# A hybrid decoder block: nine modulation sections loaded transposed and summed along the row on VectorE

## The reference, cut to what matters

```
c_act = silu(c)                                   # 1024 numbers
mod   = c_act @ w_ada + b_ada                     # nine sections of 1024
sh1, sc1, gt1, sh2, sc2, gt2, sh3, sc3, gt3 = split(mod, 9)
x = x + 0.5*gt1*swiglu(rmsnorm(x)*(1+sc1)+sh1)    # first feed-forward
x = x + gt2*mixer(rmsnorm(x)*(1+sc2)+sh2)         # attention and short convolution
x = x + 0.5*gt3*swiglu(rmsnorm(x)*(1+sc3)+sh3)    # second feed-forward
shf, scf = split(c_act @ w_ada_final + b_ada_final, 2)
out = rmsnorm(x)*(1+scf)+shf
```

## Time and profile before

| | before |
|---|---|
| median of three runs | 1863.17 us |
| profiled execution, its time | 1860.78 us |
| profiled execution, its span | 1859.0 us |
| PE busy, of the span | 1810.6 us, 97% |
| DVE busy | 1261.2 us, 68% |
| ACT busy | 774.6 us, 42% |
| bytes moved | 269.77 MB, mean 145 GB/s |
| mean granted TensorE clock | 0.996 of 2.4 GHz |

### The profile page before, as it was taken

How to read it: one execution, slowest core, us unless ns; L and a number is a source line. 1 busy time by engine, 2 the same in 40 slices (tenths; PEclk the granted TensorE clock), 3 DMA queues, 4 the chain that set the end, 5 groups by cost and what they waited for, 6 DMA issues and landing times.

```text
span 1859.0 us, 23169 instructions
## 1 busy us (share of the span) xinstructions
PE 1810.6 (97%) x8370; PEld 1472.2 (79%) x8370; DVE 1261.2 (68%) x1951; ACT 774.6 (42%) x1393; POOL 268.3 (14%) x411
## 2 busy tenths in 40 slices
PE   6999999999999999999999999999999999999997
PEld 3778888888888887888877777778888888888886
DVE  5887777777576786444326668787667666576767
ACT  5643333333344565211125666663333333344445
POOL 2011211211210000000303330201111111111000
PEclk9999999999999999999999999999999999999998
DMA  8165565665765321111211110424545545476432
GB/s 324 58 235 205 200 231 193 225 216 181 266 215 155 106 69 70 56 34 57 68 38 42 46 35 1 176 97 159 196 170 181 207 153 193 159 261 215 125 97 91
DMA packets 100529, 269.77 MB, mean 145 GB/s; under 512 B 13120, under 2 KB 13504, under 8 KB 100288
## 3 DMA queue, kind: packets, MB, share of 16 engines
q1 hardware_dynamic: 65680, 150.50, 24.0%
q0 software_dynamic: 34304, 117.46, 18.5%
q10 hardware_dynamic: 432, 0.34, 0.1%
HBM read 209.53 MB, written 54.53 MB: 142 GB/s over the span
## 4 chain that ended last, share of the span: by engine, by line
PE 86%; DVE 8%; ACT 3%; issue 1%; DMA 1%; POOL 0%; ACTq 0%; DVEq 0%; POOLq 0%
PE PS L1554 62%; PE PS L1550 23%; DVE Wl L1021 1%; DVE NMax L1463 1%; PE PS L1988 1%; DMA AdaFirst<-ada 1%; DVE X L1359 1%; DVE X L1122 1%; ACT X L701 0%; ACT Bh L701 0%; DVE CT L1428 0%; DVE Bl L1128 0%; DVE SqSum L1328 0%; DVE Ml L1262 0%; DVE TmpA L1346 0%
## 5 line engine op out<-in xcount | busy, mean ns | idle before, releaser
L1554 PE MATMUL PS<-Bh,Wh 128*128 128x512 f32 x1120 | 437.5, 391 | 4.5 <-ACT T L684 4.1
L1554 PE MATMUL PS<-Bh,Wl 128*128 128x512 f32 x1120 | 435.9, 389 | 0.0
L1554 PE MATMUL PS<-Bl,Wh 128*128 128x512 f32 x1120 | 435.8, 389 | 0.0
L1554 PEld LDWEIGHTS PS<-Bh,Wh 128*128 128x128 f32 x1120 | 210.3, 188 | 50.7 <-DVE Wl L1021 4.9
L1554 PEld LDWEIGHTS PS<-Bh,Wl 128*128 128x128 f32 x1120 | 210.2, 188 | 44.0
L1554 PEld LDWEIGHTS PS<-Bl,Wh 128*128 128x128 f32 x1120 | 210.3, 188 | 43.1
L1554 PE MATMUL PS<-Wh 128*128 128x512 f32 x616 | 240.0, 390 | 0.0
L1554 PE MATMUL PS<-Wh,Wl 128*128 128x512 f32 x616 | 239.7, 389 | 0.0
L1554 PE MATMUL PS<-Wl,Wh 128*128 128x512 f32 x616 | 239.7, 389 | 0.0
L1053 DVE TENSOR_TENSOR Wl<-RawB,Wh 128x512 fp32r<-128x512 f32 x154 | 106.5, 692 | 130.3 <-ACT Wh L659 129.3
L659 ACT ACTIVATE Wh<-RawB 128x512 fp32r<-128x512 f32 x154 | 97.3, 632 | 230.7 <-PE PS L1554 230.7
(11 more groups left out here) (201 smaller groups left out, 2872.6 us busy)
## 6 DMA issues: line engine op xcount, KB each, us to landing
Raw<-up_w SPq DMA_DIRECT2D x86, 512.0 KB, 5.3
Ada<-ada POOLq DMA_DIRECT2D x72, 512.0 KB, 4.3
g_dram<-T SPq DMA_DIRECT2D x88, 256.0 KB, 2.3
W2s<-down_w POOLq DMA_DIRECT2D x88, 256.0 KB, 4.5
s_dram<-W2s POOLq DMA_DIRECT2D x88, 256.0 KB, 2.8
GQ<-g_dram POOLq DMA_DIRECT2D x88, 256.0 KB, 3.4
RawB<-s_dram SPq DMA_DIRECT2D x88, 256.0 KB, 2.9
RawB<-down_w SPq DMA_DIRECT2D x66, 256.0 KB, 2.7
```

The costliest lines, as they stand in the source:

```text
L1554: return nc.tensor.matmul(out, lhs, rhs, start=first, stop=last, skip_group_check=True)
```

## The change

Of the nine later sections the matrix is stored transposed, so that a tile has 128 outputs on its partitions and all 1024 inputs along the row. `silu(c)` is needed along the row as well: `c`, copied to all 128 partitions, is stored behind the tiles. In each phase SP loads it into `CRow` (half a megabyte), and ACT applies Silu to it in place. `CRow` lies where `AdaSum` lay, over the second half of an operand of the plain jobs and over `Spread`, so its load waits for both. A DVE instruction per tile then multiplies tile and `CRow` and gives the sum of the products along the row as its accumulator output, straight into one column of `Mod`; the products themselves overwrite the tile. `ada_cols` goes, and with it `ada_between`. `ada_bias` adds the bias to `Mod` in place.

```diff
@@ SP, block_of
-                for q in (0, 2, 1, 3):
+                for q in (0, 2):
+                    spill(ph, 0, q)
+                sp.wait_ge(prod, N_FFN * ph + 8)
+                sp.wait_ge(bcast_done, 2 + 4 * ph)
+                sp.dma_start(CRow[:], ada[SECTIONS * KT]).then_inc(row_loaded, 16)
+                for q in (1, 3):
                     spill(ph, 0, q)
@@ ACT, up
                     if t > 10:
                         up_evict(ph, t - 1)
+                    if t == 11:
+                        act.wait_ge(row_loaded, 16 * (ph + 1))
+                        nc.scalar.activation(CRow[:], CRow[:], ACT.Silu).then_inc(c_act, 1)
@@ DVE, ada_tile
+                if s in (ADA_IN[0][0], ADA_IN[1][0]) and k == 0:
+                    dve.wait_ge(c_act, 2 if s == ADA_IN[0][0] else 3)
                 dve.wait_ge(ada_loaded[n % 2], 16 * (n // 2 + 1))
-                if k == 0:
-                    dve.wait_ge(cols_done, s + 1)
-                    nc.vector.tensor_scalar(AdaSum[:], Ada[:, n % 2, :], CAct[:, 0:1], None, ALU.mult).then_inc(ada_used, 1)
-                else:
-                    dve.wait_ge(ada_used, s * KT + k)
-                    nc.vector.scalar_tensor_tensor(AdaSum[:], Ada[:, n % 2, :], CAct[:, k:k + 1], AdaSum[:],
-                                                   ALU.mult, ALU.add).then_inc(ada_used, 1)
+                a = s * KT + k
+                nc.vector.scalar_tensor_tensor(Ada[:, n % 2, :], Ada[:, n % 2, :], 1.0, CRow[:], ALU.mult, ALU.mult,
+                                               accum_out=Mod[:, a:a + 1]).then_inc(ada_used, 1)
@@ DVE, ada_bias
-                dve.wait_ge(cols_done, s + 2 if s else 2)
+                if s:
+                    dve.wait_ge(ada_used, (s + 1) * KT)
@@ PE, up
-                    ada_between(ph, t)
@@ PE
-            def ada_cols(s, bank=7):
-
-                pe.wait_ge(ada_used, (s + 1) * KT)
-                for c in range(KT):
-                    made = mm(PS[:, bank, c:c + 1], AdaSum[:, blk(c)], Ones[:], True, True)
-                made.then_inc(cols_done, 1)
@@ arrays
-        "ada": ada_w.reshape(KT, P, SECTIONS, D).transpose(2, 0, 1, 3).reshape(SECTIONS * KT, P, D),
+        "ada": np.concatenate([ada[:2 * KT], turned[2 * KT:], np.broadcast_to(a["c"][0], (1, P, D))]),
```

More of the change, by code:

```diff
@@ L189, in program @@
         Ada, _ = place("Ada", [P, 2, D], like=z_at)
-        AdaSum, _ = place("AdaSum", [P, D], like=z_at + 8 * K)
+        CRow, _ = place("CRow", [P, D], like=z_at + 8 * K)
         W2s, _ = place("W2s", [P, 4, HALF], like=tmp_at)
@@ L359, in program @@
         mset, consts, c_act = sem("mset"), sem("consts"), sem("c_act")
+        row_loaded = sem("row_loaded")
         ada_used, row_used, row_done = sem("ada_used"), sem("row_used"), sem("row_done")
@@ L1305, in second_scale, with ada_bias @@
                                                col("g1", KH * n, KH), ALU.add, ALU.mult).then_inc(scales, 1)
-            def ada_bias(s, bank=7):
-                dve.wait_ge(cols_done, s + 2 if s else 2)
-                nc.vector.tensor_tensor(Mod[:, bass.ts(s, KT)], PS[:, bank, 0:KT], Cols[:, bass.ts(s, KT)], ALU.add)\
-                    .then_inc(mod_done, 1)
+            def ada_bias(s):
+                if s:
+                    dve.wait_ge(ada_used, (s + 1) * KT)
+                else:
+                    dve.wait_ge(cols_done, 2)
+                nc.vector.tensor_tensor(Mod[:, bass.ts(s, KT)], Mod[:, bass.ts(s, KT)] if s else PS[:, 4, 0:KT],
+                                        Cols[:, bass.ts(s, KT)], ALU.add).then_inc(mod_done, 1)
             def scale(n, section, gain):
@@ L1398, in _ @@
             second_bias(0)
-            ada_bias(SH1, 4)
+            ada_bias(SH1)
             second_scale(0)
@@ L1559, in spin @@
                     mm(PS[:, bank, HALF - P:HALF], ident, ident, True, True)
[L1561 to L1567, removed]
             def plain_group(ph):
@@ L2091 @@
     below = np.where(np.arange(P)[None, :] <= np.arange(P)[:, None], 0.0, MASKED)
+    ada = ada_w.reshape(KT, P, SECTIONS, D).transpose(2, 0, 1, 3).reshape(SECTIONS * KT, P, D)
+    turned = ada_w.T.reshape(SECTIONS * KT, P, D)
     arrays = {
```

## The result

The changed kernel took 1845.28 us (median of four runs, 1843.78 to 1846.76) against 1863.16 before (1862.52 to 1863.54): ratio 0.9904, interval 0.9887 to 0.9922, 17.9 us less. The forecast was 1848.5 with a range from 1846.5: right in direction and mechanism, too small, and the time fell out of the range at its lower end. The profiled execution took 1845.61, 15.2 less than that of before.

The account below looks back on a forecast made before the run. TensorE was taken to bound the kernel, its chain in the up projections broken only by nine blocks. -15.7 + 0.7 + 0.3 = -14.7 us, from 1863.17 to 1848.5 us; range 1846.5 to 1856.

Parts of the forecast that it names:

- mechanism: Up projections: TensorE is the unbroken chain, so matmul blocks taken out of it are time spared at the end.
- The term of the blocks: TensorE, up projections: nine column-making matmul blocks at 1.68 to 1.81 us each go, 15.7 us gained.
- the stalls: TensorE waiting for DVE sums delayed by tiles: 0.7 us at the two first tiles, 0.3 at six later places.
- The tile's growth x: DVE: the accumulator output lengthens each 1.28 us tile by 0 to 1.06 us; 0.15 taken.
- The late matmul of the earlier trace: TensorE at t = 61, first matmul of j = 6: already late behind a DVE tile and sum, slack -0.2 us.
- the slack method: Compares when DVE's sum arrives with when TensorE wants it, wherever a tile stands ahead; 1.0 us lost in all.
- The rule against this change: DVE: two non-bf16 SBUF sources halve throughput, leaving no read port for accumulator readback; the sum would be rival 1's.
- Rival 1: DVE tiles: accumulator output halves the rate, x = 1.06; net gain 8.3 us, 1855 us; chance 0.11.
- Rival 2: Up projections: the nine blocks were covered by sums or weights, two thirds of the gain lost, 1858 us; chance 0.04.
- Rival 3: Phase 0 sections: DVE ends the up projections if tiles exceed 3.2 us; at 3.6 us, 1878 us; chance 0.03.
- Rival 4: Row's load lands late and ACT stops at t = 11: +0.6 us a phase, 1850 us; within the forecast's 0.80.
- What SP, the queues and ACT get: Row load issued at about 91.3, Silu from 104.3 to 105.4, both hidden; no cost to TensorE.

Follow-up runs that it names:

- later tiles: Changed kernel with eight identity matmuls ahead of t = 12 in phase 0 alone and each phase's first tile at t = 15 instead of 12: 1842.96 us.
- gap_spin: Changed kernel with eight identity matmuls (spins) on TensorE just ahead of t = 12 in both phases: 1843.86 us.
- blocks out: Kernel before without the nine blocks, with eight identity matmuls ahead of t = 12 in both phases: 1843.19 us.
- tile_pointer: Changed kernel with the tile's constant factor 1.0 read from a column of ones: 1845.81 us.
- blocks_back: Changed kernel with the nine blocks of eight matmuls put back at their old places on TensorE, result unread: 1862.10 us.
- after: The changed kernel itself against the kernel before, first measurement and its profile: 1845.28 us.
- after_again: The changed kernel measured once more without any edit: 1846.15 us.
- blocks_out: Kernel before without the nine blocks, tiles and sums as they were, no identity matmuls: 1845.36 us.
- tile_later: Changed kernel with the first tile of each phase at t = 15 in place of 12: 1844.59 us.
- spin_first: Changed kernel with eight identity matmuls ahead of t = 12 in phase 0 alone: 1844.59 us.

## Why the prediction was right or wrong

**The mechanism was right.** The blocks lay bare on the path, and their removal is the gain: blocks put back, 1862.10; blocks alone out, 1845.36. The rest of the change takes 0.3 us of it back.

**The term of the blocks was mis-sized: this is the step that failed first.** The gain was forecast as 14.7 us and measured as 17.9. Of the 3.2 between them 0.9 is this term, 0.7 the stalls (next paragraph), and the other 1.6 is chance in the main (last two paragraphs). It says "Nine blocks are 15.1 to 16.3 us; I take 15.7", the mean of 1.68 and 1.81. But 1.68 was known to leave out the wider gap behind the block, so a mean with it had no ground. And 1.81, taken as the upper bound, was too low as well: the blocks measured 1.84 each, 16.6 us. The comparison of starts around a block gives 1.81; the missing 0.03 to 0.04 lies further back, where the matmuls stay a little too far apart for some two microseconds. In the trace of before, behind the sixth block:

```profile
470.05 0.40 PE L1554 MATMUL PS<-Bl,Wh 128*128 128x512 f32 x1
470.29 0.40 PE L1554 MATMUL PS<-Bh,Wl 128*128 128x512 f32 x1
...
472.14 0.39 PE L1554 MATMUL PS<-Bl,Wh 128*128 128x512 f32 x1
```

The last of these starts nine matmuls behind the first, 2.09 us later in place of 2.04. The trace of before would have told it: from t = 13 to its first down matmul,

```profile
486.50 0.39 PE L1554 MATMUL PS<-Wh 128*128 128x512 f32 x1
```

are 378.84 us, and 135 steps of 12 matmuls at 0.227 are 367.7. That leaves 11.1 for six blocks, about 1.85 each.

**The tile's growth x was bounded on the wrong side.** "0 to 1.06 us. I take 0.15": it is -0.06. The instruction lost the per-partition factor, and with a factor from memory it has its old 1.279 again. The accumulator's read is a separate instruction of 0.083 us, as the ACT row suggested, but the next instruction starts with it. With -0.06 the prediction's own arithmetic gives 0.20 + x = 0.14 at each first tile. Measured is 0.23 and 0.20 (table, the changed kernel with spins less that with later tiles), so the loss that was forecast there did come. The late matmul of the earlier trace rows has no counterpart with the shorter tile: from 110.9 to 469 us no two starts in `gap_spin`'s trace are more than 0.04 too far apart. That gives back 0.06 a phase (table, blocks out less later tiles); the prediction had read the lateness as 0.2. With a tile of 1.279 again, in `tile_pointer`, the same matmul is late again by 0.08. Net 0.17 and 0.15 are lost. So the slack method was about right and its input wrong: it charged 1.0 where 0.3 was lost.

**The rule against this change did not hold.** By the rule of the Trainium skill that was weighed (Vector Engine (DVE) Microarchitecture Reference, Points that are easy to get wrong) the tile would take 2.34 us, as the prediction estimated. It takes 1.219 with both sources float32 in SBUF and the accumulator in use. That such an instruction counts as two, as the Trainium skill says (VectorE: DVE Perf Modes, Two Vector instructions with no wait between them), the traces do show: 72 tiles, and 72 accumulator reads.

**The rivals.** Rival 1 was priced about right for the wrong event: a pair of 2.5 us cost 10.5, where its places would give 8.6 at x = 1.2; 1.0 of the rest came at places that it doesn't list. Rival 2 is refuted by `blocks_back`. Rival 3's point, a tile over 3.2 us, was not reached by any run; at 2.5 the kernel was still 6 us faster than before. Rival 4 did not come: the row landed in 3.6 us, and ACT did not stop for it.

**What SP, the queues and ACT get** was right: the issue at 91.33 (said: 91.3), Silu 1.05 us long (said: 1.06), and no wait of DVE for it or for `Ada`. The Silu started at 105.67 and not at 104.3, because this execution's first plain matmul came 1.4 us later than that of before.

**The range was too narrow below.** The corrected sum, -16.6 + 0.3 = -16.3, from 1863.17 gives 1846.9, inside the range. What took the time out of it, 1.6 lower, is chance in the main: by the repeats one median was 0.9 high, the other 0.9 low. The lower end of the prediction allowed 0.8 us for both, and calls it 1. Its trace of before had been of the kinder sort, with an early start and the slow stretch hidden at 55 us; one execution 2.4 below the median was a sign that single executions differ by more than 1 us. The traces show three places where executions differ whatever the kernel. The first plain matmul starts between 43.1 and 45.1 us. The slow stretch at t = 12 is long, short or not there. And from the first down matmul of phase 1 to the end it is 227.1 us in eight traces and 227.7 to 228.1 in six. What decides them was not settled.

One more difference goes with the blocks, and no term of the prediction has it. From the first down matmul of phase 0 to t = 12 of phase 1 the four traces with blocks take 767.5 to 768.0 us and the ten without 767.1 to 767.3. So 0.2 to 0.9 us of the gain lie there, outside the stretches where the blocks stand; the cause is open.

## What to carry to other kernels

Where TensorE is one unbroken chain, price a block that goes by the length of a long stretch less its matmuls at their spacing, not by the block's own row; the row leaves out the ragged restart. Bound an unseen instruction from below zero as well, and look at each operand that changes with it, constants too. Before a difference of a few microseconds is explained, see whether both traces start alike and have their clock dips in the same place.

## What the runs showed of the hardware

- A scalar_tensor_tensor of 1024 float32 took 1.219 us with a constant factor and 1.279 with one from a column; the accumulator read of 0.083 us starts together with the next instruction.
- Behind a wait of 3.7 us at t = 12, TensorE's clock was granted at 0.50 (the 1.2 GHz level) for 6 to 13 matmuls, 0.43 us apart. It was so in eight of nine traces without spins. By the first down matmul 0.8 to 2.3 us of it were left in the three traces compared here (371.94, 373.04 and 373.18 us from t = 12 in `after`, `after_again` and `blocks_out`, against 371.10 and 370.93 with spins).
- In the ninth trace the dip lay at 55 us, behind waits of 1.36 and 1.12, and was hidden. The same two waits stand in other traces without a dip at 55 us (`gap_spin`, `tile_later`), so what brings it there is open.
- With the wait cut to 1.9 by 2 us of identity matmuls (0.8 in `spin_first`) the clock stayed at 1.00 there in all five traces, though in one (spins in phase 0 alone) the dip at 55 us came again.
- With the same filling, four runs of the changed kernel lay within 0.15 us, against 2.7 without; in the four other kernels with filling the spread was 0.7 to 1.7, so 0.15 is in part luck.
